# Expert layers of a mixture-of-experts block: the bias product on 64x64 places, the token gather by 64 stationary columns

## The reference, cut to what matters

```python
logits = (h @ w_router + b_router).astype(jnp.float32)
top_val, top_idx = lax.top_k(logits, TOP_K)          # TOP_K = 4 of 32
gates = jax.nn.softmax(top_val, axis=-1)
...
def expert_block(args):                              # xblk: the tokens of expert e
    gu = xblk @ w_exp_in[e] + b_exp_in[e]            # 1024 -> 2048, with an input bias
    gate = jnp.minimum(gu[:, :D_FF], SWIGLU_LIMIT)
    up = jnp.clip(gu[:, D_FF:], -SWIGLU_LIMIT, SWIGLU_LIMIT)
    act = (up + 1.0) * gate * jax.nn.sigmoid(SWIGLU_ALPHA * gate)
    return act @ w_exp_out[e] + b_exp_out[e]         # 1024 -> 1024
```

## Time and profile before

| | us |
|---|---|
| median of 3 runs (1910.51 to 1919.05) | 1913.71 |
| the profiled execution, its own time | 1913.38 |
| span of the profiled execution | 1911.6 |
| TensorE matmuls busy | 1775.5 (93%) |
| TensorE weight loads busy | 968.8 (51%) |
| VectorE busy | 601.7 (31%) |
| ScalarE busy | 435.6 (23%) |
| GpSimd busy | 161.2 (8%) |
| mean granted TensorE clock, share of full speed | 0.974 |
| moved by DMA | 489.71 MB |

### The profile page before, as it was taken

How to read it: one execution, slowest core, us unless ns; L and a number is a source line. 1 busy time by engine, 2 the same in 40 slices (tenths; PEclk the granted TensorE clock), 3 DMA queues, 4 the chain that set the end, 5 groups by cost and what they waited for, 6 DMA issues and landing times.

```text
span 1911.6 us, 45718 instructions
## 1 busy us (share of the span) xinstructions
PE 1775.5 (93%) x20042; PEld 968.8 (51%) x20042; DVE 601.7 (31%) x1316; ACT 435.6 (23%) x726; POOL 161.2 (8%) x203
## 2 busy tenths in 40 slices
PE   5889899999999999885999999999999999999996
PEld 2356667676766676644443443434434434344342
DVE  3253737465564646325111111111111111111111
ACT  2224242423333343402111111111111111111111
POOL 0021212121212121302000000000000000000000
PEclk9989999999999999995899999999999999999998
DMA  9641112111121212006699999999999999999992
GB/s 376 252 193 37 61 37 62 48 59 56 44 60 37 68 30 79 3 1 275 243 423 426 425 427 428 428 427 428 427 427 427 428 428 428 427 427 428 427 428 114
DMA packets 75468, 489.71 MB, mean 256 GB/s; under 512 B 9632, under 2 KB 10704, under 8 KB 21440
## 3 DMA queue, kind: packets, MB, share of 16 engines
q1 hardware_dynamic: 75200, 487.46, 62.3%
q0 software_dynamic: 128, 0.11, 0.0%
HBM read 486.49 MB, written 1.05 MB: 255 GB/s over the span
## 4 chain that ended last, share of the span: by engine, by line
PE 52%; DVE 0%; ACT 0%; issue 0%; DVEq 0%; ACTq 0%
PE PS L1596 24%; PE PS L1646 12%; PE PS L1581 7%; PE PS L1588 3%; PE PS L1603 3%; PE PS L1632 1%; PE PS L1651 1%; PE PS L1619 0%; DVE MT L1741 0%; DVE MT L1743 0%; ACT MT L1684 0%; DVEq L1542 0%; DVE y L1702 0%; ACT backT L1680 0%; DVE st L1740 0%
## 5 line engine op out<-in xcount | busy, mean ns | idle before, releaser
L1596 PE MATMUL PS<-raw,hgT 128*64 128x512 f32 x2120 | 472.5, 598 | 0.0
L1596 PEld LDWEIGHTS PS<-raw,hgT 128*64 128x64 f32 x2120 | 146.8, 137 | 299.1 <-issue 299.1
L1646 PE MATMUL PS<-raw,actT 128*64 128x512 f32 x1056 | 232.2, 592 | 0.0
L772 PEld LDWEIGHTS PS<-raw 64*64 64x64 f32 x6912 | 153.5, 136 | 58.7 <-issue 43.5
L681 PE MATMUL PS<-arena 128*128 128x256 f32 x640 | 166.6, 399 | 10.4 <-ACT raw L463 10.4
L772 PE MATMUL PS<-raw 64*64 64x64 f32 x6912 | 168.9, 224 | 7.7 <-issue 4.3
L1715 DVE TENSOR_SCALAR back<-cst,now 128x128 f32<-128x128 f32 x66 | 19.8, 343 | 428.4 <-PE PS L1651 428.4
L1646 PEld LDWEIGHTS PS<-raw,actT 128*64 128x64 f32 x1056 | 75.9, 137 | 150.7 <-issue 150.7
L1581 PEld LDWEIGHTS PS<-take,MT 128*128 128x128 f32 x1088 | 127.3, 196 | 30.9 <-issue 26.8
L1723 DVE TENSOR_SCALAR gate_half<-PS 128x512 f32<-128x512 f32 x33 | 22.8, 690 | 374.6 <-PE PS L1596 374.6
L1581 PE MATMUL PS<-take,MT 128*128 128x64 f32 x1088 | 132.0, 281 | 4.0 <-DVE take L1696 4.0
(11 more groups left out here) (307 smaller groups left out, 1781.0 us busy)
## 6 DMA issues: line engine op xcount, KB each, us to landing
raw<-in_w_exp SPq DMA_DIRECT2D x397, 1024.0 KB, 10.8
arena<-in_w_blk SPq DMA_DIRECT2D x67, 512.0 KB, 3.6
raw<-in_w_ada SPq DMA_DIRECT2D x24, 1024.0 KB, 9.8
arena<-in_w_out SPq DMA_DIRECT2D x8, 512.0 KB, 3.5
arena<-in_lora_up SPq DMA_DIRECT2D x8, 192.0 KB, 4.4
arena<-in_ctx SPq DMA_DIRECT2D x2, 512.0 KB, 5.0
xl<-in_x SPq DMA_DIRECT2D x2, 512.0 KB, 6.9
out_x<-MT SPq DMA_DIRECT2D x2, 512.0 KB, 3.1
```

Of the source, the lines that this page charges most:

```text
L772: ins = mm(out[H[h ^ to], c, :], lhsT[H[h ^ at], c, :], rhs[H[h ^ at], c, :], start=start, stop=stop)
L1596: ins = mm(PS[H[h], GU + g, :], hgT[:, s, :], raw[:, s, cols], start=False, stop=s == KT - 1, skip_group_check=True)
L1646: ins = mm(PS[H[m], Y, :], aT[:, q, H[h]], raw[:, KT + q, cols], start=q == 0 and h == 0, stop=q == 3 and h == 1, skip_group_check=True)
```

## The change

Three edits belong together, and all are for the stage `experts`.

The bias. `bin_` goes from 64 rows x 2 x 512 to 128 rows x 512: rows 0 to 63 hold the gate bias (32 experts for each half of the channels), rows 64 to 127 the up bias. It is loaded by one transfer, no longer by two. `bsel` gets 128 rows, and `bias()` becomes four products of 64 rows x 64 columns, one for each g and each half. To have the one-hot code of the expert on all 128 partitions, `project` makes the counts per expert on 128 partitions (`sel2`, `more`, `ebefore`, `first`, `rank`, `base`, `inside`) where it made them on 64.

The gather. Each product with 128 stationary columns becomes two with 64, one for each half of the output partitions: 32 products for 16.

The waits. TensorE's waits for `bsel_dn` and `gu_rd` move from behind the four activation transposes to ahead of them.

```diff
-        bin_ = sb("bin", [2 * NE, 2, 512])
+        bin_ = sb("bin", [P, 512])[:, :]
...
-        sel2 = r.take(TT, 2 * NE)
+        sel2 = sq[:, 0:TT * P].rearrange("p (i n) -> p i n", n=P)
...
-            for h in range(2):
-                sp.dma_start(bin_[h * NE:(h + 1) * NE, :, :], a["b_exp_in"][h]).then_inc(bin_loaded, 16)
+            sp.dma_start(bin_, a["b_exp_in"]).then_inc(bin_loaded, 16)
...
-                    mm(PS[0:2 * NE, 4, 2 * NE:2 * NE + 1], sel2[:, 0, :], k("ones")[:, 0:1], start=True, stop=False)
+                    mm(PS[:, 4, 2 * NE:2 * NE + 1], sel2[:, 0, :], k("ones")[:, 0:1], start=True, stop=False)
...
-            mm(PS[0:2 * NE, 5, 0:1], k("ebefore")[0:NE, :], more[0:NE, :], start=True, stop=True)
+            mm(PS[:, 5, 0:1], k("ebefore")[0:NE, :], more[0:NE, :], start=True, stop=True)
...
-                ins = nc.vector.tensor_copy(sel2[:, i, 0:NE], sel[:, i, :])
-                step(nc.vector.tensor_copy(sel2[:, i, NE:2 * NE], sel[:, i, :]), S["sel_dn"])
+                step(nc.vector.tensor_copy(sel2[:, i, :].rearrange("p (q n) -> p q n", n=NE),
+                                           sel[:, i, :].unsqueeze(1).broadcast_to([P, P // NE, NE])), S["sel_dn"])
...
-        bsel = sb("bsel", [2 * NE, P])
+        bsel = sb("bsel", [P, P])
...
                 for kt in range(KT):
                     for i in range(TT):
-                        ins = mm(PS[:, HG, kt * HALF:(kt + 1) * HALF], h2[:, i, kt * P:(kt + 1) * P], take[:, i, :],
-                                 start=i == 0, stop=i == TT - 1)
+                        for h in range(2):
+                            ins = mm(PS[H[h], HG, kt * HALF:(kt + 1) * HALF], h2[:, i, kt * P + HALF * h:kt * P + HALF * (h + 1)],
+                                     take[:, i, :], start=i == 0, stop=i == TT - 1)
...
                 for g in range(2):
-                    ins = mm(PS[:, GU + g, :], bsel, bin_[:, g, :], start=True, stop=False, skip_group_check=True)
+                    for h in range(2):
+                        ins = mm(PS[H[h], GU + g, :], bsel[H[g], H[h]], bin_[H[g], :], start=True, stop=False, skip_group_check=True)
...
                 pe.wait_ge(S["act_dn"], i + 1)
+                pe.wait_ge(S["bsel_dn"], i + 2)
+                pe.wait_ge(S["gu_rd"], i + 1)
                 for q in range(4):
                     ins = nc.tensor.transpose(PS[:, TR, q * P:(q + 1) * P], ac[:, q * P:(q + 1) * P], k("ident"))
                 ins.then_inc(S["at_mm"], 1)
-                pe.wait_ge(S["bsel_dn"], i + 2)
-                pe.wait_ge(S["gu_rd"], i + 1)
                 bias()
...
-                ts(bsel, k("halves")[0:2 * NE], cur[0:2 * NE, 0, 2 * TT:2 * TT + 1], None, ALU.mult).then_inc(S["bsel_dn"], 1)
+                ts(bsel, k("halves"), cur[:, 0, 2 * TT:2 * TT + 1], None, ALU.mult).then_inc(S["bsel_dn"], 1)
```

More of the change, by code:

```diff
@@ L57 @@
 for _name, _w in (("ident", P), ("ones", P), ("heads", P), ("headmean", P), ("before", P), ("slots", P),
-                  ("cls", 4), ("who", NE), ("halves", P), ("ebefore", HALF), ("enum", 1), ("scan0", T), ("scan1", T),
+                  ("cls", 4), ("who", NE), ("halves", P), ("ebefore", P), ("enum", 1), ("scan0", T), ("scan1", T),
                   *((f"{m}{d}", C) for d in (0, 1) for m in ("nF", "eF", "nP", "sF", "iF")), ("eye", C)):
@@ L80, in constants @@
     put("who", (p[:, None] % NE == np.arange(NE)).astype(np.float32))
-    put("halves", (p[:, None] // NE == p[None] // HALF).astype(np.float32))
-    put("ebefore", (p[:, None] < np.arange(HALF)[None] % NE).astype(np.float32))
+    put("halves", (p[:, None] // NE % 2 == p[None] // HALF).astype(np.float32))
+    put("ebefore", (p[:, None] < np.arange(P)[None] % NE).astype(np.float32))
     put("enum", p[:, None] % NE)
@@ L1386, in _ @@
                 else:
-                    mm(PS[0:2 * NE, 4, 2 * NE:2 * NE + 1], sel2[:, 0, :], k("ones")[:, 0:1], start=True, stop=False)
-                    ins = mm(PS[0:2 * NE, 4, 2 * NE:2 * NE + 1], sel2[:, 1, :], k("ones")[:, 0:1], start=False, stop=True)
+                    mm(PS[:, 4, 2 * NE:2 * NE + 1], sel2[:, 0, :], k("ones")[:, 0:1], start=True, stop=False)
+                    ins = mm(PS[:, 4, 2 * NE:2 * NE + 1], sel2[:, 1, :], k("ones")[:, 0:1], start=False, stop=True)
             ins.then_inc(S["pos_mm"], 1)
             pe.wait_ge(S["more_dn"], 1)
-            mm(PS[0:2 * NE, 5, 0:1], k("ebefore")[0:NE, :], more[0:NE, :], start=True, stop=True)
+            mm(PS[:, 5, 0:1], k("ebefore")[0:NE, :], more[0:NE, :], start=True, stop=True)
             mm(PS[0:1, 6, 0:1], more[0:NE, :], k("ones")[0:NE, 0:1], start=True, stop=True).then_inc(S["start_mm"], 1)
@@ L1476, in _ @@
                 step(tt(sel[:, i, :], sel[:, i, :], eq[:, i, :], ALU.add))
-                ins = nc.vector.tensor_copy(sel2[:, i, 0:NE], sel[:, i, :])
-                step(nc.vector.tensor_copy(sel2[:, i, NE:2 * NE], sel[:, i, :]), S["sel_dn"])
+                step(nc.vector.tensor_copy(sel2[:, i, :].rearrange("p (q n) -> p q n", n=NE),
+                                           sel[:, i, :].unsqueeze(1).broadcast_to([P, P // NE, NE])), S["sel_dn"])
             nc.vector.memset(table[:, :, :], 0.0)
             step(nc.vector.memset(jobs[:, :], 0))
-            c = PS[0:2 * NE, 4, 2 * NE:2 * NE + 1]
+            c = PS[:, 4, 2 * NE:2 * NE + 1]
             dve.wait_ge(S["pos_mm"], 1)
-            step(ts(more[0:2 * NE], c, float(HALF), None, ALU.is_gt))
+            step(ts(more[0:P], c, float(HALF), None, ALU.is_gt))
             for b in (2, 3):
-                step(stt(out=more[0:2 * NE], in0=c, scalar=float(b * HALF), in1=more[0:2 * NE], op0=ALU.is_gt, op1=ALU.add),
+                step(stt(out=more[0:P], in0=c, scalar=float(b * HALF), in1=more[0:P], op0=ALU.is_gt, op1=ALU.add),
                      S["more_dn"] if b == 3 else None)
@@ L1497, in _ @@
             dve.wait_ge(S["start_mm"], 1)
-            w = slice(0, 2 * NE)
+            w = slice(0, P)
             step(ts(first[0:1], PS[0:1, 6, 0:1], float(NE), None, ALU.add))
@@ L1609, in _ @@
             gather()
-            pe.wait_ge(bin_loaded, 32)
+            pe.wait_ge(bin_loaded, 16)
             pe.wait_ge(S["bsel_dn"], 1)
@@ L1760, in layouts @@
     slots = np.concatenate([into, outof], axis=1)
-    bias = f("b_exp_in").reshape(NE, 2, 2, 512).transpose(2, 0, 1, 3)
+    bias = f("b_exp_in").reshape(NE, 2, 2, 512).transpose(1, 2, 0, 3).reshape(P, 512)
     return {
```

## The result

The changed kernel takes 1891.03 us (median of 4 runs, 1888.16 to 1892.53), the kernel before 1913.95 in the same series: ratio 0.9877, 95% interval [0.9856, 0.9897], 22.9 us less. The forecast was 1893 in 1879 to 1907.

The account below looks back on a forecast made before the run. TensorE was taken to set the pace in `experts`, with the weight stream taking over at 29.4 us a job. Lead 16.1 + hole 1.7 + start 3.0 - router 0.2 = 20.6 us off 1913.4 gave 1893 us, range 1879 to 1907.

Parts of the forecast that it names:

- The bound, and which one takes over: In `experts` TensorE sets the pace; once the lead is gone, after about 5 jobs, the stream does, 29.4 us a job.
- the rival of a stream that gives more when pressed: Weight transfers in `experts` exceed 428 GB/s: 1889 us at 430; chance 0.08 for under 1880.
- the estimate at the 435 GB/s: Weight stream at the skill's ceiling: its 385 blocks would take 928 us, giving 1878 us.
- the slower rival: Each 64-column gather load pays for 128, 1981 us, chance 0.04; or starved TensorE gets lower clock, some 1930, chance 0.04.
- TensorE's saving: Per job in `experts`: gather 1.8, step 0.5, bias 0.86, together 3.2 us, from 29.4 to 26.2.
- the step into the gather: Idle before the gather's first load falls from 0.81 to about 0.3 us: 0.5 us saved a job, bounds 0 and 0.5.
- The lead used up: End of `experts`: the last block's products begin 2.0 us behind the stream's end, giving 16.1 us.
- T + 2.0: For a stream ending at T, the last block's products begin 2.0 us later.
- The earlier start of the stream: Start of `experts`: 3.0 us from first gather and bias (bounds 0 and 5), 1.7 from the hole, router 0.2 lost.
- My fear for the clock: Start of `experts`: if the clock rises only after L1619, that group takes 6.8 us and eats 2.7.
- The hole of 1.7 us in the first turn: Stream gap at 946 to 948 us, 0.72 MB, would be filled since places come free sooner: 1.7 us gained.
- Signs that did not come: Profile after: TensorE waits for blocks in L1596 and L1646, some 3 us a job; SyncE's total waits as long as before.

Follow-up runs that it names:

- before_10: The kernel before with two of twelve weight blocks a job not transferred after the first job: 1913.27 us, ratio 1.0009.
- after_10: The changed kernel with two of twelve weight blocks a job not transferred after the first job: 1817.6 us, ratio 0.9503.
- gather_twice: The changed kernel with every gather in the loop done twice: 1894.42 us, ratio 0.9878.
- bias_only: The changed kernel with the old gather of 16 products of 128 columns: 1893.69 us, ratio 0.9905.
- gather_only: The kernel before with only the gather split into products of 64 columns, bias and waits as before: 1889.82 us, ratio 0.9886.
- ring18_order: The changed kernel with six more ring places kept in use, and blocks requested in order of need from the ninth turn: 1878.83 us, ratio 0.9805.

## Why the prediction was right

**The bound, and which one takes over: right, and shown.** `before_10` shows TensorE as the bound before, `after_10` and `gather_twice` the stream after, `bias_only` and `gather_only` that a saving of 0.9 us a job brings nearly the same end as one of 2.7. The first wait for a block comes at 1086.4 us, in the seventh turn; I had said from about the sixth job on. The rate stayed at 427 to 428 GB/s with landing times of about 25 us, so the rival of a stream that gives more when pressed is out, and with it the estimate at the 435 GB/s of the Trainium skill, DMA: Bandwidth & Descriptors, Where 436 GB/s comes from. (I had written that no window holds that rate. The 2 us from 1870 to 1872 show 438 GB/s before the change; over 750 us it is 427 in both kernels.) The granted clock stayed at its upper level through the waits (1.00 in the long window), and the loads of 64 columns do go side by side: 62 in 1.89 us, 30 ns each. Both forms of the slower rival are out.

**TensorE's saving: 3.2 us predicted, 2.74 measured** (29.40 to 26.66). The failing term is *the step into the gather*, 0.5 us. The first loads do come 0.5 us sooner, at 1416.47, 0.43 us behind the last pair of the input products. But the matmuls of the gather begin at 1416.90 only, when those products have streamed: the wait of 0.81 us before was hidden behind the same streaming. From the last pair of input loads to the scatter it took 4.67 us before and takes 2.82 now, 1.85 less for gather and step together; the bias gives 0.89 as predicted. The gather's own length fell by 3.79 - 2.03 = 1.76, so the step gave 0.09 us of its 0.5.

The drain at a change of tiling mode that the Trainium skill, TensorEngine Tiling (Array Packing), Key Properties, describes shows on one side of the new bias only: the loads stand idle for 0.81 us ahead of the input products behind it (0.76 before the change), but for 0.17 us ahead of the bias itself, as before.

```profile
1421.36 0.21 PEld L1589 LDWEIGHTS PS<-bin,bsel 64*64 64x64 f32 x8 [0.17 <-issue]
...
1422.38 0.20 PEld L1597 LDWEIGHTS PS<-raw,hgT 128*64 128x64 f32 x4 [0.81 <-issue]
```

In these timelines the long idle time at a change of shape stands only behind products that move 512 columns; those ahead of the bias are transposes that move 128. For the sum none of this mattered.

**The lead used up: 16.1 us predicted, 14.3 measured.** I let TensorE have a block when its bytes had passed. Place 7 was begun at 1856.65, 1867.1 - 1856.65 = 10.4 us ahead of the stream's end in place of 12.25: so by this estimate 1.8 us lie between the last byte of a block and the product that uses it (1.3 us by the same reckoning in the second profile). (I had also written that a block is needed 29.4 us after its request. It is the 1.9 us of its own products less, 27.5; after the change the slowest block lands after 27.0.) The formula "T + 2.0" should have been "T + 3.8"; the changed kernel, profiled again, shows 3.3, and `ring18_order` 3.9.

**The earlier start of the stream: 3.0 + 1.7 - 0.2 us predicted, 8.9 measured.** From the router's start, the stream ended at 1014.3 us before and 1005.4 after, 8.9 us sooner, and in the span 7.1, since this execution's mixer ended 1.8 later.

The start itself was sized too small, even with its bound of 5 us (half of 7.09 + 3.78 is 5.4, too, and not 5.2). The first input products begin 50.7 us after the router's start, where it was 55.5, even though the router itself took 1.1 us more (0.75 of it in its first products, which the change doesn't touch). They and the products behind them also ran faster, so that place 1's products (917.90 us, before 922.90) begin 56.2 us after the router's start for 63.0: 6.8 us sooner. My fear for the clock was unfounded here: it rose at 911.7 us, during the bias, where it had risen only at 918.6 during the input products. What the engine did before it rose is in the rows: gather in 64-column pairs, in place of 128-column products half as many. In `gather_only` it rose at 906.9 us, during the bias; in `bias_only`, with the long gather, at 912.6 us, during the first input products. In this profile it then fell once more (0.50 in 919 to 921 us), as it had at 922 before the change, and the first turn's input products take 13.93 us; in the second profile of the same kernel it did not fall, and they take 12.24.

The hole of 1.7 us in the first turn was not filled, against what I had said. It is there in the same size in both profiles, 2.0 us of stream in six (before, then after):

```profile
944.00:950.00 6.00, 6.00 (x28) 1.92 (x28) 0.00 (x0) 0.00 (x0) 0.00 (x0) 1.00 0.71 284
```

```profile
940.00:946.00 6.00, 6.00 (x29) 1.84 (x26) 0.00 (x0) 0.00 (x0) 0.00 (x0) 1.00 0.94 285
```

So 6.8 of the 8.9 us are traced to the start, none to the hole, and some 2 us are not traced to a row. The sum of 20.6 came to 21.4 in this pair of profiles by errors that offset each other: 4.4 us more at the start, 1.8 less of the lead, and 1.8 for the mixer's own shift. That the forecast is only 2 us off is in part luck; that it lies near 20 us and not near 105 is not. In the medians the gain is 22.9.

**Signs that did not come.** The output products never waited for a block, though I had named L1646. And SyncE's waits for input products did not stay as long as before: they fell from 542.4 to 228.8 us. What filled the rest of SyncE's time the waits do not name.

**Open.** Why the untouched mixer ends anywhere between 857 and 866 us was not tried. The stage times of 1028.6 and 1024.1 us of the same kernel come apart mostly before 960 us (the first profile, then the second):

```profile
906.00:960.00 54.00, 52.44 (x384) 22.13 (x386) 8.35 (x27) 6.50 (x9) 0.00 (x0) 0.92 0.76 298
```

```profile
906.00:960.00 54.00, 54.00 (x402) 22.51 (x400) 8.11 (x21) 7.69 (x11) 0.00 (x0) 0.97 0.80 324
```

26 GB/s x 54 us are 1.4 MB, 3.3 us of stream. The clock's second fall is in the first profile only and goes with it; what decides whether the clock falls there is not known.

## What to carry to other kernels

Two engines at nine tenths are not a tie to be guessed at: look which one waits for the other, and measure the lead (how long before its use a transfer lands). A saving on the engine that sets the pace counts per turn until the lead is gone, and after that only the ends of the transfer stream count: when it starts, where it has holes, and how far behind its end the last dependent work is. A deeper ring gave a clear gain here (some 13 us, by the ratios of 0.9805 and 0.9876) only when its places stayed in use and the requests went out in the order of need as well; a single use of the six places, or their use without that order, gave 5 us at most.

## What was not expected of the hardware

In the changed kernel the tail is set by the last block that TensorE has to wait for, not by the last block of the stream: 14.3 us of TensorE work covered five blocks of 2.45 us, so leaving one of them out moved nothing. The clock behaved differently in two executions of the same kernel: in the one it fell again for the first turn's input products, in the other it did not. And the idle time of 0.8 us ahead of the loads at a change of shape stands only behind products that move 512 columns.

Expected, and now measured: the eight products of a bias on 64x64 places took 1.09 us where four on 64x128 took 1.98, so all four places stream at once, with two sets of rows writing to two banks. With two places at once nothing would have been saved.
